# Two of the three column sums of each late pair move from Pool to the vector engine

## The chip, the cores and the metric

One core of a Trainium2 chip runs the whole program. The time is the device time of one execution in microseconds; the median of three runs is what is predicted. Names: TensorE (PE in the rows, PEld its weight loads), the vector engine (DVE), ScalarE (ACT), Pool (POOL), and SP, whose queue starts the DMAs.

## What is computed

A stack of four layers over 512 tokens of width 1024. The change lies in the last two layers, in the feed-forward block of each:

```python
h = rms_norm(x, norm_g[l, 2]) * (1.0 + sc2) + sh2
y = jnp.square(jax.nn.relu(h @ w_up[l])) @ w_down[l]      # w_up 1024x4096, w_down 4096x1024
x = x + gt2 * rms_norm(y, norm_g[l, 3])
```

Everything is float32, and the result must have float32's accuracy. The hidden size 4096 is the inner dimension of the product with `w_down`.

## The kernel before

Each float32 product is made of three reduced-precision ones: an operand is split into a high part (a rounded copy, made by ScalarE) and a low part (the operand less its high part, made by the vector engine), and TensorE adds high x high, low x high and high x low.

The feed-forward block of a layer runs in four chunks (`CHUNKS`, c = 0 to 3) of eight 128-wide tiles of the hidden size. In a chunk TensorE first makes the eight hidden tiles (L2551 to L2553), then the down projection of these 1024 rows of `w_down`. The down projection saves products: it is a two-by-two block product with seven multiplications in place of eight (the Winograd form), which needs sums and differences of blocks of the weights (column sums) and of the hidden activations (row sums). The seven multiplications are spread over eight steps w = 0 to 7 that the text calls pairs. Early pairs (0 to 3) and late pairs (4 to 7) have three products each, numbered i, in the order i = 2, 0, 1, each for two halves j = 0, 1, and a product is three matmuls of 128x512 (L3192 to L3194): 18 matmuls a pair. The seventh multiplication, 24 matmuls with the column differences of all late pairs (tile `col_diff`), closes the chunk.

For a late pair w the blocks of `w_down` lie in the tile `down_raw` (four blocks raw[:, 0] to raw[:, 3], one DMA of 1 MB from SP's queue, four buffers), and this is made of them:

- column difference t3 = raw3 - raw2, sum 1 = t3 + raw0, sum 2 = raw1 - sum 1: L1526, L1529 and L1532, all three on Pool, four pairs one after the other (`late_sums`). Sums 1 and 2 go to the tile `down_whole`, which shares its memory with `down_low`, so they wait for TensorE's products of pair w - 2.
- ScalarE (`late_high`, in this order): high part of raw3 (L1319), of t3 (L1321), and of both sums together, 128x1024 (L1323). It waits for the difference before the second and for sum 2 before the third.
- the vector engine: `late_block` (L2387), the low part of raw3, which product i = 2 needs; `late_low` (L2391), the low part of both sums, 128x1024, which products i = 0 and i = 1 need; and `diff_low` (L2394), the low part of t3, which only the seventh multiplication needs.

The prediction calls these three block-low, pair-low and difference-low.

The vector engine also adds finished products from PSUM to the sums in SBUF (L2400; in chunk 0 some are copies, L2402). These gathers free banks of PSUM: the two fifth sums (128x1024 each) must be done before pair 4's product i = 2, the two first sums (128x512 each; none in chunk 0, and in chunks 0 and 3 ScalarE also copies the bank, L1403) before pair 4's product i = 0; the two second sums come between pairs 6 and 7, the sixth after pair 7.

Nothing schedules this: every engine works through its own instructions in the order written, and semaphores hold it where an operand is missing. That order is the loop at the end of the vector engine's program, and the two `for` loops over w on ScalarE and Pool.

## Time and profile before

| | before |
|---|---|
| median of 3 runs | 1935.22 us (1934.49 to 1935.59) |
| profiled execution | 1937.91 us |
| its span, first to last instruction | 1936.1 us |
| TensorE matmul busy | 1843.9 us, 95% of the span |
| vector engine busy | 1439.1 us, 74% |
| ScalarE busy | 931.5 us, 48% |
| Pool busy | 277.0 us, 14% |
| granted TensorE clock, mean | 0.988 of full speed |

The first two rows are what was timed and the one execution that was profiled; 1.8 us of that execution lie outside its span. The busy rows are sums over the whole span and hide which stage waits for what; the rows shown further down come from the late pairs. In the chain of work that ended last, Pool has 5% of the span, on lines L1526, L1529 and L1532 above all; each of the eight chunks passes through them.

### The profile page before, as it was taken

How to read it: one execution, taken by the hardware profiler on the slowest of the kernel's cores; microseconds unless marked ns; L12 is line 12 of the kernel's file. 1: busy time of each engine (PE TensorE's matmuls, PEld its weight loads, DVE VectorE, ACT ScalarE, POOL GpSimd, SP SyncE). 2: the span in 40 equal slices, each digit the busy share in tenths (PEclk: the TensorE clock that was granted, in tenths of full speed). 3: DMA queues.
4: the chain of work that ended last, by engine and by line, in shares of the span. 5: the costliest groups of instructions: out<-in, count | busy, mean ns of one | idle time of the engine just before them, and what ended most of it. 6: DMA issues, size and time to landing. Idle time of an engine off the chain costs nothing.

```text
span 1936.1 us, 25511 instructions
## 1 busy us (share of the span) xinstructions
PE 1843.9 (95%) x9594; PEld 1438.4 (74%) x9594; DVE 1439.1 (74%) x2286; ACT 931.5 (48%) x1581; POOL 277.0 (14%) x194
## 2 busy tenths in 40 slices
PE   6999998999899999999999999999999999999997
PEld 3777566887566777777987777877777898778785
DVE  5797668886698897756876758684754687585878
ACT  4554544333323345466654544554455665445364
POOL 0002100000201111000013314340000003140514
PEclk9999999999999999999999999999999999999999
DMA  9466035886001452111232424232211213242432
GB/s 363 181 226 253 1 114 201 313 328 222 8 9 39 175 193 109 66 66 67 76 132 99 152 104 178 89 153 102 95 66 45 88 61 136 103 176 93 151 136 102
DMA packets 50016, 255.07 MB, mean 132 GB/s; under 512 B 5513, under 2 KB 7562, under 8 KB 31596
## 3 DMA queue, kind: packets, MB, share of 16 engines
q1 hardware_dynamic: 49900, 253.53, 35.4%
q8 instruction: 72, 1.18, 0.2%
q14 instruction: 44, 0.36, 0.1%
HBM read 251.28 MB, written 2.10 MB: 131 GB/s over the span
## 4 chain that ended last, share of the span: by engine, by line
PE 68%; DVE 16%; POOL 5%; ACT 5%; issue 4%; DMA 2%; POOLq 0%; SPq 0%; DVEq 0%; ACTq 0%
PE banks L2551 9%; PE banks L2552 9%; PE banks L2553 9%; PE banks L2921 3%; PE banks L2923 3%; PE banks L2922 3%; PE banks L2815 3%; PE banks L3192 3%; PE banks L3194 2%; PE banks L3193 2%; PE banks L2835 2%; POOL down_whole L1529 2%; POOL down_whole L1532 2%; PE banks L2736 2%; POOL col_diff L1526 2%
## 5 line engine op out<-in xcount | busy, mean ns | idle before, releaser
L2551 PE MATMUL banks<-h_high,w_high 128*128 128x512 f32 x888 | 349.7, 394 | 11.7 <-DVE w_low L1561 7.9
L2552 PE MATMUL banks<-h_low,w_high 128*128 128x512 f32 x888 | 346.6, 390 | 0.0
L2553 PE MATMUL banks<-h_high,w_low 128*128 128x512 f32 x888 | 346.5, 390 | 0.0
L2551 PEld LDWEIGHTS banks<-h_high,w_high 128*128 128x128 f32 x888 | 167.3, 188 | 53.8 <-DVE w_low L1561 12.5
L2553 PEld LDWEIGHTS banks<-h_high,w_low 128*128 128x128 f32 x888 | 167.2, 188 | 35.0
L2552 PEld LDWEIGHTS banks<-h_low,w_high 128*128 128x128 f32 x888 | 167.3, 188 | 35.0 <-issue 0.7
L1526 POOL TENSOR_TENSOR col_diff<-down_raw 128x512 f32<-128x512 f32 x32 | 53.7, 1677 | 674.8 <-DMA down_raw<-in_wd 674.8
L1576 DVE CUSTOM_DVE_ANT_0 mod_raw<-mod_raw,cond_row 128x1024 f32<-128x1024 f32 x112 | 131.5, 1219 | 2.5 <-DMA mod_raw<-in_wmod 2.4
L2921 PE MATMUL banks<-h_high,w_high 128*128 128x512 f32 x288 | 115.2, 400 | 2.5 <-DVE w_low L2025 1.7
L2923 PE MATMUL banks<-h_high,w_low 128*128 128x512 f32 x288 | 112.3, 390 | 0.0
L2922 PE MATMUL banks<-h_low,w_high 128*128 128x512 f32 x288 | 112.2, 390 | 0.0
L1561 DVE TENSOR_TENSOR w_low<-w_raw,w_high 128x1024 fp32r<-128x1024 f32 x66 | 80.6, 1221 | 41.2 <-ACT w_high L632 41.1
L3192 PE MATMUL banks<-down_high,row_sums_high 128*128 128x512 f32 x192 | 80.9, 422 | 19.7 <-DVE down_low L2391 8.6
L632 ACT ACTIVATE w_high<-w_raw 128x1024 fp32r<-128x1024 f32 x66 | 69.8, 1058 | 48.1 <-DMA w_raw<-in_wt 27.4
L2334 DVE TENSOR_TENSOR w_low<-w_raw,w_high 128x1024 fp32r<-128x1024 f32 x49 | 64.3, 1311 | 26.2 <-ACT w_high L1271 26.2
L2109 DVE TENSOR_REDUCE stats<-banks 128x2 f32<-128x1024 f32 (+3 forms) x32 | 25.6, 822 | 74.5 <-PE banks L2952 63.2
L1278 ACT ACTIVATE relu<-banks 128x512 f32<-128x512 f32 x52 | 30.9, 594 | 99.0 <-PE banks L2553 99.0
L1323 ACT ACTIVATE down_high<-down_whole 128x1024 fp32r<-128x1024 f32 x32 | 33.9, 1060 | 90.3 <-POOL down_whole L1532 90.0
L2025 DVE TENSOR_TENSOR w_low<-w_raw,w_high 128x1024 fp32r<-128x1024 f32 x38 | 47.5, 1251 | 39.9 <-ACT w_high L981 30.1
L1271 ACT ACTIVATE w_high<-w_raw 128x1024 fp32r<-128x1024 f32 x49 | 51.3, 1048 | 52.9 <-PE banks L3194 52.9
L3193 PE MATMUL banks<-down_low,row_sums_high 128*128 128x512 f32 x192 | 75.2, 391 | 0.0
L3194 PE MATMUL banks<-down_high,row_sums_low 128*128 128x512 f32 x192 | 75.1, 391 | 0.0
(590 smaller groups left out, 4617.4 us busy)
## 6 DMA issues: line engine op xcount, KB each, us to landing
w_raw<-in_wt SPq DMA_DIRECT2D x96, 1024.0 KB, 4.9
mod_raw<-in_wmod SPq DMA_DIRECT2D x128, 512.0 KB, 5.0
down_raw<-in_wd SPq DMA_DIRECT2D x32, 1024.0 KB, 7.2
down_raw<-in_wd SPq DMA_DIRECT2D x32, 768.0 KB, 4.2
mod_first<-in_wmod SPq DMA_DIRECT2D x8, 1024.0 KB, 10.6
cmp_w<-in_cmp_w SPq DMA_DIRECT2D x4, 1024.0 KB, 6.9
x<-in_xT SPq DMA_DIRECT2D x2, 1024.0 KB, 6.6
dft<-in_dft SPq DMA_DIRECT2D x2, 1024.0 KB, 7.5
```

Of the source, the lines that this page charges most:

```text
L1526: gp.tensor_tensor(t3[:, :], raw[:, 3, :], raw[:, 2, :], sub).then_inc(*did(f"mix_s.{c}.{w}.0"))
L1561: v.tensor_tensor(low[:, :, :].rearrange("p k c -> p (k c)"), RAW[b // 2][:, b % 2, :], high[:, :, :].rearrange("p k c -> p (k c)").bitcas ...
L1576: v.tensor_tensor_reduce(w, w, row[:, :], 1.0, 0.0, mul, add, sums[:, k:k + 1]).then_inc(mod_used, 1)
L2551: mm(out, high[:, k, :], H[:, k, :], start=k == order[0], stop=False)
L2552: mm(out, high[:, k, :], L[:, k, :], start=False, stop=False)
L2553: last = mm(out, low[:, k, :], H[:, k, :], start=False, stop=k == order[-1])
L2921: mm(out, WH[t % 2][:, k, :], Hh[:, k, :], start=k == 0, stop=False)
L2922: mm(out, WH[t % 2][:, k, :], Hl[:, k, :], start=False, stop=False)
L2923: last = mm(out, WL[t % 2][:, k, :], Hh[:, k, :], start=False, stop=k == KT - 1)
L3192: mm(out, rh, wh, start=start, stop=False)
L3193: mm(out, rh, wl, start=False, stop=False)
L3194: return mm(out, rl, wh, start=False, stop=stop)
```

## The change

Pool keeps the first of its three instructions for each late pair, the column difference (`late_diff`). The two sums are now issued by the vector engine, in a new function with the old name. In the vector engine's order they stand right behind `late_block` of the same pair, and `diff_low` is moved to stand behind them, ahead of `late_low`; it now waits for ScalarE's copy of the difference by a wait of its own. For pair 4 all this comes ahead of the fifth sums. The operands, the tiles and what is computed stay the same, and TensorE, ScalarE and SP issue what they did.

```diff
-            def late_sums(c, w):
-                raw, t3, out = BLOCKS[RAW_OF[w]], T3f[w % PK], OPf[w % 2]
+            def late_diff(c, w):
+                raw, t3 = BLOCKS[RAW_OF[w]], T3f[w % PK]
                 pool.wait_ge(*when(f"blocks{RAW_OF[w]}.{c}.{w}"))
...
                 gp.tensor_tensor(t3[:, :], raw[:, 3, :], raw[:, 2, :], sub).then_inc(*did(f"mix_s.{c}.{w}.0"))
-                pool.wait_ge(*when(f"mix_s.{c}.{w}.0"))
-                pool.wait_ge(*when(f"mix_p.{c}.{w - 2}.0.1"))
-                gp.tensor_tensor(out[:, 0, :], t3[:, :], raw[:, 0, :], add).then_inc(*did(f"mix_s.{c}.{w}.1"))
-                pool.wait_ge(*when(f"mix_s.{c}.{w}.1"))
-                pool.wait_ge(*when(f"mix_p.{c}.{w - 2}.1.1"))
-                gp.tensor_tensor(out[:, 1, :], raw[:, 1, :], out[:, 0, :], sub).then_inc(*did(f"mix_s.{c}.{w}.2"))
...
                 for w in range(PK, 8):
-                    late_sums(c, w)
+                    late_diff(c, w)
...
+            def late_sums(c, w):
+                raw, t3, out = BLOCKS[RAW_OF[w]], T3f[w % PK], OPf[w % 2]
+                dve.wait_ge(*when(f"mix_s.{c}.{w}.0"))
+                dve.wait_ge(*when(f"mix_p.{c}.{w - 2}.0.1"))
+                v.tensor_tensor(out[:, 0, :], t3[:, :], raw[:, 0, :], add).then_inc(*did(f"mix_s.{c}.{w}.1"))
+                dve.wait_ge(*when(f"mix_s.{c}.{w}.1"))
+                dve.wait_ge(*when(f"mix_p.{c}.{w - 2}.1.1"))
+                v.tensor_tensor(out[:, 1, :], raw[:, 1, :], out[:, 0, :], sub).then_inc(*did(f"mix_s.{c}.{w}.2"))
...
             def diff_low(c, w):
+                dve.wait_ge(*when(f"mix_h.{c}.{w}.1"))
...
                 late_block(c, 4)
+                late_sums(c, 4)
+                diff_low(c, 4)
                 for j in range(2):
                     fifth_sum(c, j)
                 late_low(c, 4)
                 for j in range(2):
                     first_sum(c, j)
-                diff_low(c, 4)
                 for w in range(5, 8):
                     late_block(c, w)
+                    late_sums(c, w)
+                    diff_low(c, w)
                     late_low(c, w)
-                    diff_low(c, w)
```

How the instructions stand on the vector engine in chunk 1, from block-low of pair 4 to pair-low of pair 5, before the change (`y_tokens` from banks are the fifth sums, `sq` from banks the first sums):

```order
L2387 TENSOR_TENSOR down_low_200<-down_raw_218,down_high_198 128x512 [waits mix_on_scalar]
L2400 TENSOR_TENSOR y_tokens_220<-y_tokens_220,banks 128x2x512 [waits y_on_vector,mix_on_tensor] x2
L2391 TENSOR_TENSOR down_low_200<-down_whole_202,down_high_198 128x1024 [waits mix_on_scalar]
L2400 TENSOR_TENSOR sq_118<-sq_118,banks 128x512 [waits y_on_scalar,mix_on_tensor]
L2400 TENSOR_TENSOR sq_119<-sq_119,banks 128x512 [waits y_on_scalar,mix_on_tensor]
L2394 TENSOR_TENSOR col_diff_low_208<-col_diff_212,col_diff_high_204 128x512
L2387 TENSOR_TENSOR down_low_201<-down_raw_217,down_high_199 128x512 [waits mix_on_scalar]
L2391 TENSOR_TENSOR down_low_201<-down_whole_203,down_high_199 128x1024 [waits mix_on_scalar]
```

and the same stretch after it, where the line numbers have shifted (block-low is L2390, the sums L2383 and L2386, difference-low L2398, pair-low L2394, the gathers L2404):

```order
L2390 TENSOR_TENSOR down_low_200<-down_raw_218,down_high_198 128x512 [waits mix_on_scalar]
L2383 TENSOR_TENSOR down_whole_202<-col_diff_212,down_raw_218 128x512 [waits mix_on_tensor,mix_on_gpsimd]
L2386 TENSOR_TENSOR down_whole_202<-down_raw_218,down_whole_202 128x512 [waits mix_on_tensor,mix_on_vector]
L2398 TENSOR_TENSOR col_diff_low_208<-col_diff_212,col_diff_high_204 128x512 [waits mix_on_scalar]
L2404 TENSOR_TENSOR y_tokens_220<-y_tokens_220,banks 128x2x512 [waits y_on_vector,mix_on_tensor] x2
L2394 TENSOR_TENSOR down_low_200<-down_whole_202,down_high_198 128x1024 [waits mix_on_scalar]
L2404 TENSOR_TENSOR sq_118<-sq_118,banks 128x512 [waits y_on_scalar,mix_on_tensor]
L2404 TENSOR_TENSOR sq_119<-sq_119,banks 128x512 [waits y_on_scalar,mix_on_tensor]
L2390 TENSOR_TENSOR down_low_201<-down_raw_217,down_high_199 128x512 [waits mix_on_scalar]
L2383 TENSOR_TENSOR down_whole_203<-col_diff_213,down_raw_217 128x512 [waits mix_on_tensor,mix_on_gpsimd]
L2386 TENSOR_TENSOR down_whole_203<-down_raw_217,down_whole_203 128x512 [waits mix_on_tensor,mix_on_vector]
L2398 TENSOR_TENSOR col_diff_low_209<-col_diff_213,col_diff_high_205 128x512 [waits mix_on_scalar]
```

Three instructions have come between block-low of pair 4 and the fifth sums, one of them with a wait for Pool.

On Pool, pairs 4 and 5 of the same chunk before the change:

```order
L1526 TENSOR_TENSOR col_diff_212<-down_raw_218 128x512 [waits mix_on_tensor,hid_on_vector,blocks2]
L1529 TENSOR_TENSOR down_whole_202<-col_diff_212,down_raw_218 128x512 [waits mix_on_tensor,mix_on_gpsimd]
L1532 TENSOR_TENSOR down_whole_202<-down_raw_218,down_whole_202 128x512 [waits mix_on_tensor,mix_on_gpsimd]
L1526 TENSOR_TENSOR col_diff_213<-down_raw_217 128x512 [waits mix_on_tensor,blocks1]
L1529 TENSOR_TENSOR down_whole_203<-col_diff_213,down_raw_217 128x512 [waits mix_on_tensor,mix_on_gpsimd]
```

and after it, pair 4 of chunk 1 to pair 4 of chunk 2:

```order
L1526 TENSOR_TENSOR col_diff_212<-down_raw_218 128x512 [waits mix_on_tensor,hid_on_vector,blocks2]
L1526 TENSOR_TENSOR col_diff_213<-down_raw_217 128x512 [waits mix_on_tensor,blocks1]
L1526 TENSOR_TENSOR col_diff_214<-down_raw_216 128x512 [waits mix_on_tensor,blocks0]
L1526 TENSOR_TENSOR col_diff_215<-down_raw_219 128x512 [waits mix_on_tensor,blocks3]
L1526 TENSOR_TENSOR col_diff_212<-down_raw_218 128x512 [waits mix_on_tensor,hid_on_vector,blocks2]
```

The four differences of a chunk now stand back to back, each held only by its block's DMA and, for pairs 6 and 7, by the first product of pair 3.

## Rows read from the trace of the kernel before

**Rows 1.** The waits between 1085 and 1125 us: waiting, awaited, total us, times, longest

```profile
ACT down_high L1323 <- POOL down_whole L1532: 12.2, 4, 3.3
```

**Rows 2.** The timeline of TensorE, chunk 1, pair 4 and pair 7: start us, us

```profile
1103.86 0.39 PE L3192 MATMUL banks<-down_high,row_sums_high 128*128 128x512 f32 x1
...
1104.99 0.39 PE L3194 MATMUL banks<-down_high,row_sums_low 128*128 128x512 f32 x1
1105.72 0.47 PE L3192 MATMUL banks<-down_high,row_sums_high 128*128 128x512 f32 x1 [0.35 <-DVE sq L2400]
...
1121.61 0.50 PE L3192 MATMUL banks<-down_high,row_sums_high 128*128 128x512 f32 x1
```

**Rows 3.** The timeline of Pool, chunk 1, pairs 4 to 7

```profile
1097.77 1.78 POOL L1526 TENSOR_TENSOR col_diff<-down_raw 128x512 f32<-128x512 f32 x1 [64.47 <-DMA down_raw<-in_wd]
...
1101.33 1.30 POOL L1532 TENSOR_TENSOR down_whole<-down_raw,down_whole 128x512 f32<-128x512 f32 x1
...
1107.89 1.75 POOL L1526 TENSOR_TENSOR col_diff<-down_raw 128x512 f32<-128x512 f32 x1
1109.72 2.15 POOL L1529 TENSOR_TENSOR down_whole<-col_diff,down_raw 128x512 f32<-128x512 f32 x1
1111.95 1.62 POOL L1532 TENSOR_TENSOR down_whole<-down_raw,down_whole 128x512 f32<-128x512 f32 x1
1113.53 1.74 POOL L1526 TENSOR_TENSOR col_diff<-down_raw 128x512 f32<-128x512 f32 x1
```

**Rows 4.** The timeline of the vector engine, chunk 1, pairs 4 and 5

```profile
1098.39 1.71 DVE L2387 TENSOR_TENSOR down_low<-down_raw,down_high 128x512 fp32r<-128x512 f32 x1
1100.66 2.35 DVE L2400 TENSOR_TENSOR y_tokens<-y_tokens,banks 128x1024 f32<-128x1024 f32 x2 [0.56 <-PE banks L3194]
1103.76 1.23 DVE L2391 TENSOR_TENSOR down_low<-down_whole,down_high 128x1024 fp32r<-128x1024 f32 x1 [0.74 <-ACT down_high L1323]
1104.90 1.28 DVE L2400 TENSOR_TENSOR sq<-sq,banks 128x512 f32<-128x512 f32 x2
...
1109.05 1.66 DVE L2391 TENSOR_TENSOR down_low<-down_whole,down_high 128x1024 fp32r<-128x1024 f32 x1 [0.58 <-ACT down_high L1323]
1110.64 1.78 DVE L2394 TENSOR_TENSOR col_diff_low<-col_diff,col_diff_high 128x512 fp32r<-128x512 f32 x1
```

**Rows 5.** The timeline of ScalarE, chunk 1, pair 5

```profile
1107.96 1.06 ACT L1323 ACTIVATE down_high<-down_whole 128x1024 fp32r<-128x1024 f32 x1 [3.20 <-POOL down_whole L1532]
```

**Rows 6.** DMA issues, 1098 to 1099 us (pair 7's block): KB, us to landing

```profile
down_raw<-in_wd SPq DMA_DIRECT2D x1, 1024.0 KB, 6.6
```

**Rows 7.** Chunks 2 and 3: SP's request, its landing, and the timeline of TensorE

```profile
1185.42 0.33 SPq L614 DMA_DIRECT2D down_raw<-in_wd  x1
...
down_raw<-in_wd SPq DMA_DIRECT2D x1, 1024.0 KB, 6.9
...
1190.89 0.39 PE L3194 MATMUL banks<-down_high,row_sums_low 128*128 128x512 f32 x1
1191.35 0.47 PE L3192 MATMUL banks<-down_high,row_sums_high 128*128 128x512 f32 x1
...
1207.23 0.50 PE L3192 MATMUL banks<-down_high,row_sums_high 128*128 128x512 f32 x1
...
1278.23 0.47 PE L3192 MATMUL banks<-down_high,row_sums_high 128*128 128x512 f32 x1 [0.70 <-ACT sq L1403]
...
1293.48 0.50 PE L3192 MATMUL banks<-down_high,row_sums_high 128*128 128x512 f32 x1
```

**Rows 8.** Chunk 0: the timeline of Pool, the vector engine and TensorE

```profile
1011.22 2.86 POOL L1526 TENSOR_TENSOR col_diff<-down_raw 128x512 f32<-128x512 f32 x1 [167.77 <-DMA down_raw<-in_wd]
...
1012.24 0.69 DVE L2387 TENSOR_TENSOR down_low<-down_raw,down_high 128x512 fp32r<-128x512 f32 x1
...
1019.23 0.50 PE L3192 MATMUL banks<-down_high,row_sums_high 128*128 128x512 f32 x1 [0.24 <-DVE down_low L2391]
...
1035.70 0.50 PE L3192 MATMUL banks<-down_high,row_sums_high 128*128 128x512 f32 x1
```

## The prediction

> **What bounds the kernel now.** I read the table of busy shares first: TensorE is busy 95% of the span, so a change elsewhere gains only where TensorE stands still. Then the list of waits over the down projection of the first layer's chunk 1 [rows 1]: ScalarE waits 12.2 us for Pool's third column sum, more than anything waits for anything else inside the late pairs. That chain (Pool's three sums, ScalarE's high parts, the vector engine's low parts, TensorE) paces the late pairs 4 to 7. TensorE's own rows give the size [rows 2]. Undisturbed, matmuls start (1104.99 - 1103.86) / 5 = 0.226 us apart. From the first matmul of pair 4 to the product of pair 7 that uses its column sums there are 60 matmuls, 13.6 us of work, and they take 1121.61 - 1103.86 = 17.75 us. So 4.1 us are lost in this chunk, and some 33 us in eight chunks (two layers of four): that is the ceiling of a gain.
>
> **Why a pair takes 5.6 us.** Pool starts one pair's first difference at 1107.89 and the next one's at 1113.53: a period of 5.64 us [rows 3]. TensorE needs 18 x 0.226 = 4.08 us for a pair. Pool's rows alternate with the vector engine's. L2391 alone takes 1.23 us [rows 4] and a 128x512 one such as L2387 0.69 [rows 8]; beside Pool L2391 takes 1.66 and L2394 1.78 [rows 4]. The ends show the pattern: L2391 ends at 1110.71, Pool's L1529, issued at 1109.72, ends 1.16 later at 1111.87, L2394, issued at 1110.64, ends 0.55 later at 1112.42, Pool's L1532 another 1.15 later. Only one of the two engines runs such an instruction at a time. One pair holds this turn for 3 x 1.15 + 2 x 0.55 + 1.08 = 5.63 us, which is the period. The gathers from PSUM are free of it: two of 128x1024 take 2.35 us at 1100.66 while Pool works [rows 3, 4].
>
> **Part 1, pairs 5 to 7: a gain.** The vector engine now runs per pair: block-low (L2387 of before), sum 1, sum 2, difference-low, pair-low. Of independent ones the next starts 0.08 before the last ends: the two at 1104.90 take 0.68 each and 1.28 together [rows 4], so those of 0.68 us start 0.60 apart. Sum 2 needs sum 1's result: 0.68 + 0.04 = 0.72. After sum 2 ScalarE makes the high part in 1.06 [rows 5], with 0.03 and 0.04 of handing over, while difference-low runs. Pair-low (1.23) then occupies 1.14 until the next start (1103.76 to 1104.90, rows 4). The period is 0.60 + 0.72 + 0.68 + 0.03 + 1.06 + 0.04 + 1.14 = 4.27 us, if Pool's differences are out of the way. The pair-low of a pair ends 4.36 after its block-low starts. The two second-sum gathers between pairs 6 and 7 add 1.20. So the product with pair 7's sums starts 2 x 4.27 + 1.20 + 4.36 + 0.05 = 14.15 us after pair 5's block-low starts. Three saved periods are worth 3 x 1.36 = 4.1 us; but the gathers, which Pool's pace hid before, now count.
>
> **Part 2, pair 4: a loss.** Here two sums and a wait for Pool are put ahead of the gathers, and TensorE needs the gathers' bank for its very first product of pair 4. Chunk 1, on the clock of before: Pool's first difference ends at 1099.55 (1097.77 + 1.78) and block-low at 1100.10 (1098.39 + 1.71) [rows 3, 4]. Sum 1 follows to 1100.70. Pool, rid of its sums, goes straight to pair 5's difference, whose block I take as landed; it has its turn 1100.70 to 1101.85, so sum 2 ends at 1102.40. Difference-low ends at 1103.00, the two fifth sums run 1102.92 to 1105.27. TensorE wanted pair 4 at 1103.86; it starts its first product at 1104.15, its second at 1105.3 and is done with both at 1106.1. Meanwhile pair 7's block lands: it is requested as pair 4's block-low begins (1098.4) and takes 6.6 us [rows 6], so Pool's last difference asks at 1105.05, just ahead of pair-low at 1105.19. Pool goes first, to 1106.35, and pair-low ends at 1107.43. The first of the two first sums frees the next bank at 1108.03, and TensorE goes on at 1108.08, where before it did at 1105.72 [rows 2]: 2.36 us later.
>
> **Sum per chunk.** Chunk 1: pair 5's block-low starts at 1107.35 + 1.20 = 1108.55; plus 14.15 gives 1122.70 against 1121.61 [rows 2]: +1.1 us. After that product nothing in the chunk differs, since the sixth sums and the products of the column differences wait for it in both, so this is the chunk's whole change. Chunk 2: the last block is requested at 1185.42 and takes 6.9 [rows 7], to 1192.3, after pair-low has begun (about 1191.1); one turn fewer, which is 1.03 us (1106.35 less the 1105.32 at which pair-low would have had the turn). The delay at pair 4 is 2.36 - 1.03 + 0.27 (before stood less there: 1190.89 to 1191.35 against 1104.99 to 1105.72, rows 2 and 7) = 1.6; from there 14.7 instead of 1207.23 - 1191.35 = 15.88 [rows 7]: +0.4. Chunk 3: ScalarE copies bank A twice behind the first sums, in both kernels, so the delay at pair 4 is that of chunk 2, 1.6; but the copies (0.6 each) also stand ahead of pair 5's high part, and from pair 4's product on it is 14.15 + 0.47 + 0.65 = 15.3 against 1293.48 - 1278.23 = 15.25 [rows 7]: +1.7. Chunk 0: Pool's first difference took 2.86 and ended at 1014.08 [rows 8]. Sum 1 waits for it, then the same row of events, with two of Pool's differences in between and the fifth sums last at 1020.6, puts TensorE at 1021.77 against 1019.23: +2.5. There are no first sums in this chunk, so 14.05 follow against 1035.70 - 1019.23 = 16.47: +0.1. One layer: 0.1 + 1.1 + 0.4 + 1.7 = 3.3; I take the second as the first: 6.6 us. SP's queue is not in it: its block loads for pairs 5 to 7 wait for early pairs, the next weights for difference-low of pair 6, which comes earlier. The added wait for ScalarE before difference-low costs nothing: that copy is done two instructions before.
>
> The profiled execution was 1937.91 (span 1936.1), the median of the runs 1935.22; the sum goes on both: 1944.5 profiled, **1941.8** for the median.
>
> **Against two rules of the Trainium skill.** Pool's difference in chunk 0 was issued at 1011.22, while a 128x512 vector instruction that began at 1012.24 still went ahead of it [rows 8]. "SBUF — State Buffer", section "Who interferes with whom", says that whoever starts first gets the shared port pair for the whole instruction. The rows of chunk 1 agree with it; this one doesn't. By that rule the difference would here end 1.2 us sooner, the sums of chunk 0 with it, and the total would be 6.6 - 2 x 1.2 = 4.2: 1939.4. "Perfetto Trace Analysis", section "Optimizing Scalar/DVE Operations", says that moving work between the two engines might not help, as they share a read port. In this kernel the turn per pair falls from 5.63 to 1.15 + 4 x 0.55 + 1.08 = 4.43 us, so it helps in the steady pairs; that the total doesn't gain comes from the order at pair 4.
>
> **Rivals.**
> - *Gain wins (faster).* The cost at pair 4 hangs on Pool's differences getting turns between the vector engine's instructions. If the blocks land so that all of them fall under gathers from PSUM or waits, chunk 1 and chunk 0 lose two turns of 1.03 each, chunks 2 and 3 one: six a layer, twelve in all, -12.4. 6.6 - 12.4 = -5.8: 1929.4. It decides from about seven turns saved. For it: gathers and Pool do run side by side [rows 3, 4]. Against: the vector engine has no gap between 1098.4 and 1105.
> - *Draw.* Four or five of the twelve turns go that way, above all the near tie of 0.14 us at 1105.05 to 1105.19: 6.6 - 5 = +1.6, 1936.8.
> - *One more turn a chunk (slower still).* A difference blocked at pair 4 comes again before block-low of pair 5: +8 x 1.03, 1950.
> - *First come, first served in chunk 0 too:* 1939.4, as above.
>
> **How the numbers follow.** Forecast 0.53; draw 0.23; gain wins 0.12; first come 0.05; one more turn 0.07. This kernel's measurement tells about 0.2% (3.9 us) from no change, so same is 1931.4 to 1939.1. The forecast case itself reaches from 1938 to 1946; 0.02 of it falls in same. Faster 0.12, same 0.25, slower 0.63. The range leaves out the two outer cases (0.19): 1933 to 1946.5.
>
> **What would show it.** Right: Pool's rows at L1526 only, some of them above 1.3 us; pairs 5 to 7 at a period near 4.3 us; TensorE at pair 4 waiting for fifth sums and then about 2 us for pair-low; the chunk's product with pair 7's sums about 1 us later than before. Wrong: pair-low of pair 4 ending within 1 us of its old place (then the gain wins), or a period of the steady pairs above 4.6 us (then it is slower than 1945). It also fails if the chunk's loss is taken up later, by a wait of TensorE in the next chunk that shrinks; I see none there.

## The result: 6.7 us slower, and the profile after

| | before | after |
|---|---|---|
| median of 7 runs each | 1935.62 us | 1942.36 us |
| lowest to highest | 1934.49 to 1938.26 | 1939.93 to 1943.77 |
| profiled execution, its span | 1937.91, 1936.1 us | 1943.77, 1941.9 us |
| TensorE's time lost in the late pairs, eight chunks | 34.1 us | 41.0 us |
| granted TensorE clock, mean | 0.988 | 0.984 |

The ratio is 1.0030, with a 95% interval from 1.0021 to 1.0039. The "time lost" is the measure of the rest of this document: from TensorE's timeline, every distance between two starts of matmuls that is over 0.25 us, less the undisturbed 0.227 us, summed over the 30.5 us ahead of each chunk's first product with the column differences.

From the page of the kernel after (busy times, then the shares of the chain that ended last, then two groups of instructions with busy us, mean ns, and idle time before them with what ended it):

```profile
PE 1844.7 (95%) x9594; PEld 1446.0 (74%) x9594; DVE 1442.4 (74%) x2350; ACT 929.3 (48%) x1581; POOL 160.4 (8%) x130
...
PE 70%; DVE 19%; ACT 5%; issue 4%; DMA 1%; POOL 0%; SPq 0%; DVEq 0%; ACTq 0%; POOLq 0%
...
L1526 POOL TENSOR_TENSOR col_diff<-down_raw 128x512 f32<-128x512 f32 x32 | 51.5, 1611 | 751.2 <-DMA down_raw<-in_wd 708.4
...
L1323 ACT ACTIVATE down_high<-down_whole 128x1024 fp32r<-128x1024 f32 x32 | 34.0, 1061 | 93.8 <-DVE down_whole L2386 93.8
```

Pool's busy time fell by 117 us and it left the chain (5% to 0%), but the vector engine, with 64 more instructions, has only 3 us more busy time: its new instructions took the place of stretching by Pool: the median block-low went from 1.77 to 0.68 us, and the median difference-low too. What ScalarE waits for changed its name, not its size: the third sum, now the vector engine's L2386, where it was Pool's with 12.2 us in [rows 1]. The same view for the late pairs of that chunk, 1100 to 1125 us (waiting, awaited, total us, times, longest):

```profile
ACT down_high L1323 <- DVE down_whole L2386: 12.9, 4, 5.0
```

The vector engine in chunk 1, pairs 4 to 7, where [rows 4] stood (start us, us):

```profile
1097.97 1.72 DVE L2390 TENSOR_TENSOR down_low<-down_raw,down_high 128x512 fp32r<-128x512 f32 x1
1099.61 0.68 DVE L2383 TENSOR_TENSOR down_whole<-col_diff,down_raw 128x512 f32<-128x512 f32 x1
1100.33 1.76 DVE L2386 TENSOR_TENSOR down_whole<-down_raw,down_whole 128x512 f32<-128x512 f32 x1
1102.01 0.68 DVE L2398 TENSOR_TENSOR col_diff_low<-col_diff,col_diff_high 128x512 fp32r<-128x512 f32 x1
1102.61 2.34 DVE L2404 TENSOR_TENSOR y_tokens<-y_tokens,banks 128x1024 f32<-128x1024 f32 x2
1104.88 1.21 DVE L2394 TENSOR_TENSOR down_low<-down_whole,down_high 128x1024 fp32r<-128x1024 f32 x1
1106.01 1.27 DVE L2404 TENSOR_TENSOR sq<-sq,banks 128x512 f32<-128x512 f32 x2
1107.21 0.68 DVE L2390 TENSOR_TENSOR down_low<-down_raw,down_high 128x512 fp32r<-128x512 f32 x1
...
1110.34 1.23 DVE L2394 TENSOR_TENSOR down_low<-down_whole,down_high 128x1024 fp32r<-128x1024 f32 x1 [0.52 <-ACT down_high L1323]
...
1114.63 1.23 DVE L2394 TENSOR_TENSOR down_low<-down_whole,down_high 128x1024 fp32r<-128x1024 f32 x1 [0.53 <-ACT down_high L1323]
```

Pool in the same stretch, where [rows 3] stood:

```profile
1100.26 1.29 POOL L1526 TENSOR_TENSOR col_diff<-down_raw 128x512 f32<-128x512 f32 x1 [1.11 <-DMA down_raw<-in_wd]
...
1105.18 2.04 POOL L1526 TENSOR_TENSOR col_diff<-down_raw 128x512 f32<-128x512 f32 x1 [1.17 <-DMA down_raw<-in_wd]
```

And TensorE, where [rows 2] stood:

```profile
1103.97 0.47 PE L3198 MATMUL banks<-down_high,row_sums_high 128*128 128x512 f32 x1 [0.36 <-DVE y_tokens L2404]
...
1106.83 0.47 PE L3198 MATMUL banks<-down_high,row_sums_high 128*128 128x512 f32 x1 [0.86 <-DVE sq L2404]
...
1121.39 0.50 PE L3198 MATMUL banks<-down_high,row_sums_high 128*128 128x512 f32 x1 [1.11 <-DVE down_low L2394]
```

The pair-lows of pairs 5 and 6 start 4.29 us apart instead of 5.64. The entry is what got longer: TensorE waits for the fifth sums at 1103.97, for the first sums at 1106.83, and again ahead of 1121.39.

By chunk, TensorE's time lost:

| us | layer 1: chunk 0 | 1 | 2 | 3 | layer 2: chunk 0 | 1 | 2 | 3 | sum |
|---|---|---|---|---|---|---|---|---|---|
| before | 5.22 | 4.08 | 3.86 | 3.88 | 5.25 | 3.90 | 4.10 | 3.84 | 34.1 |
| after | 5.46 | 4.37 | 4.56 | 5.50 | 5.51 | 5.70 | 4.39 | 5.56 | 41.0 |
| change | +0.2 | +0.3 | +0.7 | +1.6 | +0.3 | +1.8 | +0.3 | +1.7 | +6.9 |
| forecast | +0.1 | +1.1 | +0.4 | +1.7 | +0.1 | +1.1 | +0.4 | +1.7 | +6.6 |

### The profile page after: what moved, and what is told of

Its sections match the earlier page's. It is cut to its first block, busy times and chain, and to the rows that moved or that the text cites. A ratio compares the mean times of both kernels' runs of the same rounds, so it can differ in the third digit from the quotient of the medians.

```text
span 1941.9 us, 25511 instructions
## 1 busy us (share of the span) xinstructions
PE 1844.7 (95%) x9594; PEld 1446.0 (74%) x9594; DVE 1442.4 (74%) x2350; ACT 929.3 (48%) x1581; POOL 160.4 (8%) x130
## 4 chain that ended last, share of the span: by engine, by line
PE 70%; DVE 19%; ACT 5%; issue 4%; DMA 1%; POOL 0%; SPq 0%; DVEq 0%; ACTq 0%; POOLq 0%
PE banks L2557 9%; PE banks L2559 9%; PE banks L2558 9%; PE banks L3198 3%; PE banks L2927 3%; PE banks L3200 3%; PE banks L3199 3%; PE banks L2929 3%; PE banks L2928 3%; PE banks L2821 3%; PE banks L2841 2%; PE banks L2742 2%; DVE mod_raw L1570 1%; PE banks L2956 1%; DVE down_low L2394 1%
## 5 line engine op out<-in xcount | busy, mean ns | idle before, releaser
L1526 POOL TENSOR_TENSOR col_diff<-down_raw 128x512 f32<-128x512 f32 x32 | 51.5, 1611 | 751.2 <-DMA down_raw<-in_wd 708.4
```

## Experiments

The theory: Pool's turns pace pairs 5 to 7 and their removal gains there, but at pair 4 the sums on the vector engine come into the one path that TensorE waits for. The rival theories are with each experiment. The lost time is split where pair 4's first product with its column sums starts: "to pair 4" is what lies ahead of that, "behind" what follows. Each time is compared with runs of the kernel before on the same chip (medians 1937.36, 1936.35, 1937.03 and 1937.17 us).

| kernel | median us | against before | ratio, 95% interval | lost to pair 4 | lost behind | both | between chunks |
|---|---|---|---|---|---|---|---|
| before | | | | 5.3 | 28.8 | 34.1 | 1.2 |
| after | 1942.36 | +6.7 | 1.0030 [1.0021, 1.0039] | 21.2 | 19.8 | 41.0 | 1.2 |
| pair 4 back on Pool | 1940.31 | +3.0 | 1.0017 [1.0008, 1.0026] | 5.7 | 32.3 | 38.0 | 1.2 |
| Pool without its reads | 1923.56 | -13.8 | 0.9930 [0.9917, 0.9943] | 5.4 | 18.0 | 23.4 | 1.2 |
| pair 4 alone on the vector engine | 1934.73 | -2.6 | 0.9988 [0.9980, 0.9997] | 19.6 | 10.7 | 30.3 | 1.2 |
| difference on the vector engine too | 1949.58 | +12.2 | 1.0066 [1.0053, 1.0079] | 9.0 | 39.5 | 48.5 | 1.1 |
| after, difference-lows late | 1928.73 | -7.6 | 0.9962 [0.9948, 0.9975] | 13.7 | 12.4 | 26.1 | 2.2 |
| pair 4 on Pool, difference-lows late | 1928.83 | -7.5 | 0.9964 [0.9952, 0.9976] | 6.7 | 20.1 | 26.8 | 2.2 |
| pairs 4 and 7 on the vector engine | 1927.71 | -8.6 | 0.9961 [0.9947, 0.9974] | 16.8 | 7.6 | 24.4 | 3.8 |
| filler matmuls | 1942.62 | +6.3 | 1.0031 [1.0020, 1.0042] | 16.4 | 11.8 | 28.2 | 1.2 |
| before, difference-lows late | 1935.48 | -1.6 | 0.9993 [0.9984, 1.0002] | 6.6 | 22.9 | 29.5 | 4.7 |
| fifth sums first | 1949.87 | +12.8 | 1.0067 [1.0055, 1.0079] | 30.0 | 19.0 | 49.0 | 1.2 |
| before, weights asked for earlier | 1934.45 | -2.7 | 0.9982 [0.9972, 0.9992] | 7.5 | 22.9 | 30.4 | 2.3 |
| split, difference-lows in the wait | 1931.30 | -5.9 | 0.9970 [0.9959, 0.9980] | 16.9 | 13.2 | 30.1 | 1.1 |

The change of the two right columns together gives that of the median within about 2 us in all rows but two. With the fillers it leaves out the fillers' own time, 48 x 0.227 = 10.9 us. Pool without its reads gained 3 us more than it shows, and the cause of that stays open.

### 1. Pair 4 back on Pool

Pool makes all three sums of pair 4, the vector engine has its old order there; pairs 5 to 7 as in the kernel after.

```diff
-                late_sums(c, 4)
-                diff_low(c, 4)
                 for j in range(2):
                     fifth_sum(c, j)
                 late_low(c, 4)
                 for j in range(2):
                     first_sum(c, j)
+                diff_low(c, 4)
```

> The changed kernel with pair 4 undone: pair 4's two sums are back on Pool and the vector engine has the old order there; pairs 5 to 7 stay as changed. My theory (the loss is made at pair 4, where two sums, a wait for Pool and Pool's turns at the vector engine come ahead of the gathers; pairs 5 to 7 gain): TensorE reaches pair 4's first sums product about where the kernel before did, one turn later at most (+1.1 us); from there 15.2 us follow in place of 15.9, so about +0.4 us a chunk, +3.5 us against before, 3 us less than the changed kernel. Rival (every sum on the vector engine costs the same wherever it stands): six of eight sums are still there, +5.0 us.

Measured: +3.0 us in the medians, +3.3 by the ratio; my number, though the interval (+1.5 to +5.0) just takes in the rival's +5.0. The loss didn't go, it moved by one pair. TensorE at pair 5 of chunk 1, and the vector engine ahead of it:

```profile
1103.29 0.69 DVE L2409 TENSOR_TENSOR col_diff_low<-col_diff,col_diff_high 128x512 fp32r<-128x512 f32 x1
1103.89 0.69 DVE L2401 TENSOR_TENSOR down_low<-down_raw,down_high 128x512 fp32r<-128x512 f32 x1
1104.49 1.79 DVE L2394 TENSOR_TENSOR down_whole<-col_diff,down_raw 128x512 f32<-128x512 f32 x1
...
1108.13 1.23 DVE L2405 TENSOR_TENSOR down_low<-down_whole,down_high 128x1024 fp32r<-128x1024 f32 x1 [0.52 <-ACT down_high L1323]
```

```profile
1106.90 0.39 PE L3216 MATMUL banks<-down_high,row_sums_low 128*128 128x512 f32 x1
1109.41 0.80 PE L3214 MATMUL banks<-down_high,row_sums_high 128*128 128x512 f32 x1 [2.13 <-DVE down_low L2405]
```

TensorE stood 2.51 us between these two starts, where it stood 0.99 in the kernel before. Pool, working ahead of the vector engine, had the sums of the next pair ready; the vector engine begins them only when it has finished the pair ahead. So the first pair whose sums are on the vector engine pays an entry, be it pair 4 or pair 5: the time lost up to pair 4's sums falls to 5.7 us, near the 5.3 of before, and that behind it rises from 19.8 to 32.3.

### 2. Pool without its reads

Pool's difference is a fill with zeros: same wait, same write, no operand is read. The column difference is left out of the computation here.

```diff
-                gp.tensor_tensor(t3[:, :], raw[:, 3, :], raw[:, 2, :], sub).then_inc(*did(f"mix_s.{c}.{w}.0"))
+                gp.memset(t3[:, :], 0.0).then_inc(*did(f"mix_s.{c}.{w}.0"))
```

> The changed kernel, but Pool fills the column difference with zeros in place of subtracting two blocks: the difference is left out of the computation, every wait and every other instruction stays. Pool then writes and reads nothing. My theory (turns between the two engines, taken by Pool's reading instructions, make a good part of the loss): no vector instruction is stretched beside Pool any more; 1 to 3 us less a chunk than the changed kernel, -9 us against before. The Trainium skill (SBUF: State Buffer, section Who interferes with whom) says that a vector instruction with two SBUF inputs contends only with a Pool instruction that reads SBUF; by it the rows of 0.68 us stay at 0.68. Rival (the vector engine's load alone): as the changed kernel, +6.7 us.

Measured: -13.8 us against before (I had -9), so 20 less than the kernel after. The vector engine at pair 4 of chunk 1, and one of Pool's fills under it:

```profile
1094.70 0.69 DVE L2383 TENSOR_TENSOR down_whole<-col_diff,down_raw 128x512 f32<-128x512 f32 x1
1095.43 0.69 DVE L2386 TENSOR_TENSOR down_whole<-down_raw,down_whole 128x512 f32<-128x512 f32 x1
1096.04 0.68 DVE L2398 TENSOR_TENSOR col_diff_low<-col_diff,col_diff_high 128x512 fp32r<-128x512 f32 x1
```

```profile
1095.93 0.53 POOL L1526 MEMSET col_diff<- 128x512 f32 x1 [1.95 <-DMA down_raw<-in_wd]
```

The fill ran from 1095.93 to 1096.46 beside two instructions that kept their 0.69 and 0.68; in the kernel after the row at this place took 1.76. So the entry's cost is the turns that Pool's differences take, together with the time of the differences themselves (1.79 against 0.53). All of the entry goes with them: the time lost up to pair 4's sums is 5.4 us, against 21.2 in the kernel after and 5.3 before. The Trainium skill, "SBUF — State Buffer", section "Who interferes with whom", says that a vector instruction with two operands in SBUF contends with a Pool instruction that reads SBUF, and not with one that only writes it; the trace agrees.

### 3. Pair 4 alone on the vector engine

On Pool, and on the vector engine (in its loop over pairs 5 to 7 the sums are gone):

```diff
                     late_diff(c, w)
+                    if w in (5, 6, 7):
+                        late_sums(c, w)
...
                 for w in range(5, 8):
                     late_block(c, w)
-                    late_sums(c, w)
-                    diff_low(c, w)
                     late_low(c, w)
+                    diff_low(c, w)
```

> The other part alone: pair 4's sums on the vector engine in the new order, pairs 5 to 7 with all three instructions on Pool in the old one. My theory: pair 4 is late by some 2 us as in the changed kernel, but Pool, rid of pair 4's sums, starts pair 5 so much earlier that the old pace of 5.64 us ends near the old place: -1.4 us against before (-4 to +3). Rival (every sum on the vector engine costs the same): two of eight, +1.7 us.

Measured: -2.6 us (-2.3 by the ratio); the sign and, within the interval, the size of the theory. The rival, that every sum on the vector engine costs the same (+1.7), falls. Pool goes ahead with pair 5 while the vector engine does pair 4, and pair 5's pair-low follows pair 4's by 3.15 us (1103.14 to 1106.29) where it took 5.29 before. Up to pair 4's sums this kernel loses nearly what the kernel after does (19.6 against 21.2 us), so the prediction's "part 2, a loss" stands; but behind them it loses 10.7 against 19.8. In the order that the change chose, pair 4 on the vector engine is a loss on the whole where pair 5 must follow on the same engine, and not where it doesn't.

```profile
1103.14 1.43 DVE L2405 TENSOR_TENSOR down_low<-down_whole,down_high 128x1024 fp32r<-128x1024 f32 x1
...
1106.29 1.21 DVE L2405 TENSOR_TENSOR down_low<-down_whole,down_high 128x1024 fp32r<-128x1024 f32 x1
```

### 4. The difference on the vector engine too

```diff
                 late_block(c, 4)
+                late_diff(c, 4)
                 late_sums(c, 4)
```

and the same for pairs 5 to 7; Pool does nothing in the late pairs.

> One step further: the column difference too goes to the vector engine, right behind block-low; Pool has nothing in the late pairs. My theory (the vector engine's own work ahead of the gathers counts; the turns are only part): its period is 0.6 longer, 4.9 us, so 2 us more in pairs 5 to 7, less what the turns cost at pair 4: +9.6 us against before. Rival (turns alone are the loss): without Pool there are none and the kernel is faster than before, some -5 us.

Measured: +12.2 us, 2.6 more than I had. No row is stretched any more, but the chain of one pair has a fifth instruction in it: the pair-lows of pairs 5 and 6 start 5.01 us apart. An instruction of 0.69, whose result the next one needs, makes every pair 0.72 us longer; on Pool the four differences took turns around pair 4 alone. There this kernel loses only 9.0 us, 12 less than the kernel after, so most of the entry of 16 us was turns; behind it it loses 20 more.

```profile
1109.51 1.23 DVE L2403 TENSOR_TENSOR down_low<-down_whole,down_high 128x1024 fp32r<-128x1024 f32 x1 [0.53 <-ACT down_high L1323]
...
1114.52 1.23 DVE L2403 TENSOR_TENSOR down_low<-down_whole,down_high 128x1024 fp32r<-128x1024 f32 x1 [0.53 <-ACT down_high L1323]
```

### 5. After, with the difference-lows late

The sums stay where the change put them. Difference-low of pair 4 goes into the wait for ScalarE at pair 5, the second sums into the one at pair 6, difference-low of pair 5 into that of pair 7, the last two behind everything.

```diff
-                diff_low(c, 4)
...
+                late_block(c, 5)
+                late_sums(c, 5)
+                diff_low(c, 4)
+                late_low(c, 5)
+                late_block(c, 6)
+                late_sums(c, 6)
+                for j in range(2):
+                    second_sum(c, j)
+                late_low(c, 6)
+                late_block(c, 7)
+                late_sums(c, 7)
+                diff_low(c, 5)
+                late_low(c, 7)
+                diff_low(c, 6)
+                diff_low(c, 7)
```

> The changed kernel with only the vector engine's order altered: difference-low of pair 4 goes from ahead of the fifth sums into pair 5's wait for ScalarE, difference-low of 5 into pair 7's, those of 6 and 7 to the end, and the second sums into pair 6's wait. Pool and the split of the work stay as changed. My theory (the changed kernel loses by what stands ahead of the gathers and of pair-low, not by who adds): pair-low of pair 4 ends 0.6 us sooner, the second sums cost nothing: 1 to 2 us less a chunk than the changed kernel, -7 us against before. Rival (the load counts, wherever it stands): as the changed kernel, +6.7 us.

Measured: -7.6 us, my number, 14 less than the kernel after, with the same instructions on the same engines. Half of the gain lies up to pair 4's sums (13.7 us lost instead of 21.2), where difference-low no longer stands ahead of the fifth sums, and half behind them (12.4 instead of 19.8). The second sums now lie under ScalarE's high part:

```profile
1110.60 0.69 DVE L2386 TENSOR_TENSOR down_whole<-down_raw,down_whole 128x512 f32<-128x512 f32 x1
1111.21 1.28 DVE L2404 TENSOR_TENSOR y_tokens<-y_tokens,banks 128x512 f32<-128x512 f32 x2
1112.42 1.22 DVE L2394 TENSOR_TENSOR down_low<-down_whole,down_high 128x1024 fp32r<-128x1024 f32 x1
```

The pair-lows of pairs 6 and 7 start 4.28 apart (1112.42 to 1116.70), where the kernel after has 5.48 (1114.63 to 1120.11).

### 6. Pair 4 on Pool, difference-lows late

Experiments 1 and 5 together: the difference-lows and second sums as in experiment 5, and at pair 4

```diff
-                late_sums(c, 4)
                 for j in range(2):
                     fifth_sum(c, j)
                 late_low(c, 4)
```

> The same order, and pair 4's two sums back on Pool. My theory: -10 us against before, 3 us less than the one with pair 4 on the vector engine. Rival (load): +5 us.

Measured: -7.5 us, 2.5 short, and no better than experiment 5. The two gains don't add: TensorE still waits 2 us or so at pair 5 (1107.60 to 1109.53 in chunk 1), the entry of experiment 1.

### 7. Pairs 4 and 7 on the vector engine, 5 and 6 on Pool

On Pool, and the vector engine's order (the first line taken out stood ahead of the fifth sums, the rest stands behind the first sums):

```diff
                     late_diff(c, w)
+                    if w in (5, 6):
+                        late_sums(c, w)
...
-                diff_low(c, 4)
...
-                for w in range(5, 8):
...
+                late_block(c, 5)
+                late_low(c, 5)
+                late_block(c, 6)
+                late_low(c, 6)
+                late_block(c, 7)
+                late_sums(c, 7)
+                diff_low(c, 4)
+                for j in range(2):
+                    second_sum(c, j)
+                late_low(c, 7)
+                diff_low(c, 5)
+                diff_low(c, 6)
+                diff_low(c, 7)
```

> The sums divided: pairs 4 and 7 on the vector engine, 5 and 6 on Pool, with three of the differences' low parts at the end of the late pairs. Pool, free of pair 4, is early with pair 5's sums, so both engines bring pairs in turn. My theory: 1.2 to 2 us less a chunk than before, -14 us. Rival (load): four of eight sums, +3.3 us.

Measured: -8.6 us (-7.6 by the ratio), the fastest median of all kernels that compute the whole result, though its interval overlaps those of experiments 5 and 6, and 5 to 6 short of my number. The late pairs gave 9.7 us; 2.6 were lost again between the chunks, and in three chunks a stretch at TensorE's lower clock came behind a wait of 2 us (below).

### 8. Filler matmuls

After the change TensorE's matmuls start 0.427 us apart for about 4 us behind its longest waits. Six matmuls without use are put into the wait at pair 4, and the wait that guards their bank goes ahead of them.

```diff
-                        if i == 1 and w == PK:
+                        if i == 0 and w == PK:
                             pe.wait_ge(taken, U + PER_CHUNK * c + 8 + PRIME)
+                            for _ in range(6):
+                                mm(bank(BANK_F), A2h[:, 1, 0, 0:P], A2h[:, 1, 0:2, :].rearrange("p n c -> p (n c)"), start=True, stop=True)
```

> The changed kernel with six matmuls of 128x512 (1.4 us, into a bank that is free there) put into TensorE's wait between pair 4's first products and its sums' products. In the changed kernel's trace some chunks show matmuls 0.427 us apart in place of 0.227 for some 4 us behind a wait of 2 us or more. My theory: in these chunks TensorE waits for pair 5's pair-low anyway, so the slower stretch costs nearly nothing; with the filler the 0.427 go away in the chunks whose wait lies there, and the time stays within 2 us of the changed kernel (+5 to +9 against before). Rival (the slower stretch adds 0.2 us a matmul to the chunk, about 2 us in each of five chunks): up to 10 us less than the changed kernel, -3 against before.

Measured: +6.3 us, the time of the kernel after, as the theory said; the rival (-3) falls. The wide spacing was gone in chunks 1 to 3 of both layers and the time didn't move. In two of them where the spacing had been wide, and where one turn fell at pair 4 with the fillers as without (chunk 2, and chunk 3 of the second layer), the lost time with the fillers' own 1.36 us is 4.3 and 5.5 us, against 4.6 and 5.5 in the kernel after. So there the slow stretch costs next to nothing: TensorE would wait for pair 5's pair-low anyway.

### 9. Before, with the difference-lows late

All sums on Pool, and only the vector engine's order changed (against the kernel before).

```diff
-                diff_low(c, 4)
-                for w in range(5, 8):
...
+                late_block(c, 5)
+                late_low(c, 5)
+                late_block(c, 6)
+                late_low(c, 6)
+                for j in range(2):
+                    second_sum(c, j)
+                late_block(c, 7)
+                diff_low(c, 4)
+                late_low(c, 7)
+                diff_low(c, 5)
+                diff_low(c, 6)
+                diff_low(c, 7)
```

> All three sums of every late pair stay on Pool, as in the kernel before; the only change is in the vector engine's order: each pair's difference-low runs later, where the vector engine would otherwise stand waiting for ScalarE (the last three of them behind pair 7's pair-low), and the second sums likewise. My theory: where difference-low stands is a lever of its own, because it then takes no turn from Pool's sums while TensorE waits for them; my schedule gives -6 us against before (about 1930). Rival: the gain of the version with this order and the sums on the vector engine came from the move of the sums alone; then this is 0 +- 2 against before, since Pool's three turns a pair still pace pairs 5 to 7 (period near 5.6 less 0.5 at most).

Measured: -1.6 us, 0.9993 [0.9984, 1.0002]: no difference that can be told. That is the rival's number, and the period is the rival's too (5.6 less 0.5 at most): it fell from 5.64 to 5.20. What neither had is that this was a gain, given back elsewhere:

```profile
1106.49 1.29 POOL L1526 TENSOR_TENSOR col_diff<-down_raw 128x512 f32<-128x512 f32 x1
1107.86 2.17 POOL L1532 TENSOR_TENSOR down_whole<-col_diff,down_raw 128x512 f32<-128x512 f32 x1
1110.11 1.62 POOL L1535 TENSOR_TENSOR down_whole<-down_raw,down_whole 128x512 f32<-128x512 f32 x1
1111.69 1.29 POOL L1526 TENSOR_TENSOR col_diff<-down_raw 128x512 f32<-128x512 f32 x1
```

The late pairs lost 4.6 us less. 3.5 of them were given back between the chunks, in the hidden tiles of the next one:

```profile
1224.25 0.39 PE L2572 MATMUL banks<-h_high,w_low 128*128 128x512 f32 x1
1225.93 0.47 PE L2570 MATMUL banks<-h_high,w_high 128*128 128x512 f32 x1 [1.29 <-issue]
```

SP asks for the next chunk's weights after pair 6's difference-low. That request came 1.68 us ahead of the chunk's first product with the column differences, where the kernel before has 6.41.

### 10. Before, with the weights asked for earlier

Experiment 9 with pair 6's difference-low in the place of pair 4's.

```diff
                 late_block(c, 7)
-                diff_low(c, 4)
+                diff_low(c, 6)
                 late_low(c, 7)
+                diff_low(c, 4)
                 diff_low(c, 5)
-                diff_low(c, 6)
                 diff_low(c, 7)
```

> The version with all sums on Pool and late difference-lows, with one more swap: pair 6's difference-low takes the place of pair 4's (ahead of pair 7's pair-low, no longer behind it). SP requests the next chunk's first weights only after pair 6's difference-low. Theory: late difference-lows shortened the late pairs by 4.6 us in eight chunks (TensorE's lost time 34.1 to 29.5) and gave 3.5 back, since the request came at 1120.62 in chunk 1 instead of 1118.07 and TensorE then waited in the next hidden tiles (4.7 us between the chunks instead of 1.2). With the request back near 1118 the 3.5 are kept: 1935.5 - 3.5 = 1932. Rival: the time between the chunks has nothing to do with the request (code or another block): 1935.5 +- 1.5 as before the swap.

Measured: -2.7 us (-3.5 by the ratio). The request came 4.70 us ahead, and the time between the chunks fell from 4.7 to 2.3 us: the cause is the request, and two thirds of what I expected came back. One chunk lost a turn instead, so the total moved by 1 to 2 us, which the two intervals don't tell apart.

### 11. The fifth sums first

```diff
                 late_block(c, 4)
+                for j in range(2):
+                    fifth_sum(c, j)
                 late_sums(c, 4)
                 diff_low(c, 4)
-                for j in range(2):
-                    fifth_sum(c, j)
```

> The changed kernel with one change: at pair 4 the two fifth sums come ahead of the two column sums and of difference-low (block-low, fifth sums, sum 1, sum 2, difference-low, pair-low). My theory: the column sums then end later and ScalarE's high part with them, which nothing covers any more, so pair-low of pair 4 comes about 1.3 us later than in the changed kernel in every chunk while TensorE's first product of pair 4 is no longer late; +1.0 to +1.3 a chunk, +8 to +10 us over the changed kernel (about 1951). Rival: the fault of the change is that it put three instructions ahead of the gathers; putting the gathers back in front then gives back what pair 4 lost, -4 to -7 us against the changed kernel (1935 to 1938, no slower than before).

Measured: +12.8 us, 6 more than the kernel after; the theory said 8 to 10, the rival a gain. TensorE has its bank at once, runs on, and then stands 4.02 us:

```profile
1102.44 0.39 PE L3200 MATMUL banks<-down_high,row_sums_low 128*128 128x512 f32 x1
1106.46 0.76 PE L3198 MATMUL banks<-down_high,row_sums_high 128*128 128x512 f32 x1 [3.63 <-DVE sq L2404]
```

From Pool's first difference to this product it is 10.51 us (1095.95 to 1106.46), in the kernel after 9.48 (1097.35 to 1106.83). So the order at pair 4 that the change chose is the better of the two, and the loss doesn't come from the fifth sums standing behind the column sums. With the fifth sums first, the column sums end later, and pair-low waits 0.52 us for ScalarE's high part, which the fifth sums covered in the kernel after.

### 12. The split, with difference-lows in the wait

In experiment 7 the vector engine stands idle for 4.37 us ahead of pair 6's pair-low.

```diff
                 late_block(c, 6)
+                diff_low(c, 4)
+                diff_low(c, 5)
                 late_low(c, 6)
                 late_block(c, 7)
                 late_sums(c, 7)
-                diff_low(c, 4)
+                diff_low(c, 6)
                 for j in range(2):
                     second_sum(c, j)
                 late_low(c, 7)
-                diff_low(c, 5)
-                diff_low(c, 6)
                 diff_low(c, 7)
```

> The fastest version so far (sums of pairs 4 and 7 on the vector engine, of 5 and 6 on Pool), with the difference-lows of pairs 4 and 5 put into the vector engine's 4.4 us wait ahead of pair 6's pair-low, and pair 6's ahead of pair 7's pair-low, so that SP's request for the next weights comes about 3.5 us earlier. Theory: the 3.8 us between the chunks go back to 1.2 and the late pairs stay at 24.4: 1927.7 - 2.6 = 1925, low enough to beat every version. Rival: the two instructions put into the wait take turns from Pool's second sum of pair 6, which ScalarE and pair-low wait for: +1.08 in each chunk, +8.6 less 2.6, so 1933 to 1934.

Measured: -5.9 us, nearer to the rival and 2 to 3 worse than experiment 7. The two intervals overlap, but the time lost in the late pairs went from 24.4 to 30.1 us. The idle time was Pool's turn. The vector engine and Pool at pair 6 of chunk 1:

```profile
1108.25 3.48 DVE L2409 TENSOR_TENSOR col_diff_low<-col_diff,col_diff_high 128x512 fp32r<-128x512 f32 x2
1111.65 1.21 DVE L2405 TENSOR_TENSOR down_low<-down_whole,down_high 128x1024 fp32r<-128x1024 f32 x1
```

```profile
1107.86 1.62 POOL L1535 TENSOR_TENSOR down_whole<-down_raw,down_whole 128x512 f32<-128x512 f32 x1
1109.44 1.75 POOL L1526 TENSOR_TENSOR col_diff<-down_raw 128x512 f32<-128x512 f32 x1
```

Two instructions of 0.68 took 3.48 us and stretched Pool's two from 1.30 to 1.62 and 1.75. The time between the chunks did go back, from 3.8 to 1.1.

## Why the prediction was right, step by step

The mechanism held, in both of its parts. Up to pair 4's first product with its sums the prediction's terms give 2 x (2.5 + 2.4 + 1.6 + 1.6), about +16 us, and behind it about -9.5; measured +15.9 and -9.0. That the single chunks add up so well is in part luck, as the steps show.

- **What bounds it.** The 4.1 us lost in chunk 1 and the chain behind them hold: in the table the time follows TensorE's lost time in the late pairs in every kernel.
- **Part 1, the steady pairs.** Forecast a period of 4.27 us, measured 4.29; from pair 5's block-low to the product with pair 7's sums forecast 14.15, measured 14.18 (1107.21 to 1121.39). The turn explains both directions: experiment 2 (no turn, no stretching) and experiment 12 (two more turns).
- **Part 2, pair 4.** Forecast that TensorE goes on with the sums' product 2.36 us later in chunk 1; measured by the time lost up to there, 1.5 in the first layer (2.00 against 0.50) and 3.1 in the second (3.30 against 0.22). This is the term that was off. In the first layer the cause is one step: "pair 7's block ... takes 6.6 us, so Pool's last difference asks at 1105.05, just ahead of pair-low at 1105.19". In the kernel after the block took 7.1:

```profile
down_raw<-in_wd SPq DMA_DIRECT2D x1, 1024.0 KB, 7.1
```

  Pool asked at 1105.18, pair-low had begun at 1104.88, and it was Pool that waited (2.04 instead of 1.29). In the second layer the tie fell as the prediction had it: Pool asked first, at 1726.23, and pair-low took 2.08.

```profile
1726.51 2.08 DVE L2394 TENSOR_TENSOR down_low<-down_whole,down_high 128x1024 fp32r<-128x1024 f32 x1
```

  The 0.7 us too little there have another cause. Pool's first difference, issued at 1718.65, let two instructions of the vector engine pass, as in chunk 0, so sum 1 waited for it and TensorE lost 0.95 us at the fifth sums in place of 0.52; and the kernel before had stood 0.3 us less at this place than in the first layer.

```profile
1721.20 1.80 DVE L2383 TENSOR_TENSOR down_whole<-col_diff,down_raw 128x512 f32<-128x512 f32 x1 [1.18 <-POOL col_diff L1526]
```

  The prediction had the near tie among its rivals ("draw") but in the sum it gave both layers the same outcome. The errors, -0.8 and +0.7, come from two different places, and that they cancelled is luck.
- **Chunk 3** (+1.7; measured +1.6 and +1.7) and **chunk 0** (+0.1; +0.2 and +0.3) came as worked out, chunk 0 with Pool's first difference losing its turn again (2.9 and 2.8 us later at pair 4 where 2.5 were forecast, and 13.7 instead of 14.05 us from there). So the first-come rival is out: Pool's difference, issued at 1010.57, let the vector engine's next two instructions go ahead, and sum 1 began only at 1013.62:

```profile
1011.76 0.68 DVE L2390 TENSOR_TENSOR down_low<-down_raw,down_high 128x512 fp32r<-128x512 f32 x1
1013.62 1.76 DVE L2383 TENSOR_TENSOR down_whole<-col_diff,down_raw 128x512 f32<-128x512 f32 x1 [1.18 <-POOL col_diff L1526]
```

  **Chunk 2** was forecast +0.4 and measured +0.7 and +0.3, but not with the turns of the forecast. In the first layer sum 2 lost no turn (0.69), and pair-low lost one (2.32) to Pool's third difference, issued 0.04 us ahead of it. In the second layer neither lost one; sum 1 of pair 5 did (1.78).
- **The two rules of the Trainium skill.** That whoever starts first gets the port pair ("SBUF — State Buffer", "Who interferes with whom") doesn't fit Pool's first row of chunk 0 after the change either, nor that of chunk 1 in the second layer, and fits the tie of pair 4 in both layers. That moving work between these two engines might not help ("Perfetto Trace Analysis", "Optimizing Scalar/DVE Operations"): it lost 6.7 us in one order and gained 7.6 in another.
- **What the profile was to show.** Pool's rows at L1526 only, several above 1.3 us (mean 1.61): yes. Waits for the fifth sums, then for pair-low: yes, save that chunk 2 has none for the fifth sums, and the second one 0.9 to 2.1 us where about 2 were named. The wrong signs, pair-low of pair 4 within 1 us of its old place or a period above 4.6, didn't show, save in chunk 2 of layer 2, where the sums' product came only 0.45 us later than before. No chunk's loss was taken up later.
- **The rivals.** "Gain wins" needed seven turns saved; against the forecast one was saved in chunk 1 of the first layer, and one in chunk 2 of the second, where it came back at pair 5. "One more turn a chunk" showed in that chunk alone. The sum of +6.6 stands against +6.9 in the lost time, +5.8 in the spans and +6.7 in the medians.
- **What was too coarse.** The prediction ascribed the loss to three instructions ahead of the fifth sums. It isn't their place there: putting the fifth sums first loses more (experiment 11, 30.0 us up to pair 4's sums in place of 21.2). The loss there is mostly turns: 5.4 us with Pool's reads gone (experiment 2), 9.0 with the difference on the vector engine (experiment 4). And whether a loss at pair 4 is paid back is decided behind it. Experiments 3 and 7 lose 19.6 and 16.8 us there and are faster than before all the same, since Pool makes pair 5's sums meanwhile; with pair 4 back on Pool (experiment 1) the loss moves to pair 5. What costs, in the order that the change chose, is the first pair that has both its own sums and its successor's on the vector engine. The order of the rest counts as much: with the difference-lows and the second sums put off, the same move of sums gains 7.6 us (experiment 5). Neither does it alone: the move alone is +6.7, the late difference-lows alone -1.6. What the second sums give by themselves no run shows; experiment 9 left them between pairs 6 and 7.

## What to carry to other kernels

When two engines take turns, as the vector engine and Pool do here, count a move in turns as well as in busy time, and then ask what the slower engine did ahead of need: work moved from an engine that ran ahead to one that works pair by pair comes onto the path once per entry into the stage. Fill the waits of the engine that got the work with whatever nobody is waiting for, but look first whether that idle time is the other engine's turn, and which later DMA request hangs on the instruction that is put off. A near tie of 0.1 us between two engines should enter a sum as half of each outcome.

## What the runs showed of the hardware that I had not expected

**TensorE's clock behind a wait.** In chunk 2 of the kernel after TensorE stood from 1190.66 to 1192.94, and from the fourth matmul behind it they started 0.43 us apart:

```profile
1193.48 0.57 PE L3200 MATMUL banks<-down_high,row_sums_low 128*128 128x512 f32 x1
1193.85 0.63 PE L3198 MATMUL banks<-down_high,row_sums_high 128*128 128x512 f32 x1
1194.28 0.63 PE L3199 MATMUL banks<-down_low,row_sums_high 128*128 128x512 f32 x1
```

The granted clock from 1189 to 1191 us and behind that wait. Each row has the stretch and its length, the busy us and instructions of PE, PEld, DVE, ACT and POOL, the granted clock (1.00, then 0.58), the DMA share and GB/s:

```profile
1189.00:1191.00 2.00, 2.00 (x10) 1.35 (x8) 2.00 (x2) 0.51 (x1) 1.18 (x1) 1.00 0.31 131
1192.90:1196.90 4.00, 3.96 (x11) 3.13 (x12) 3.44 (x6) 1.45 (x2) 0.65 (x1) 0.58 0.00 0
```

That is the lower of its two levels, 1.2 GHz, for most of the stretch, and full speed again from 1197. Five of the eight chunks of the kernel after show it. It isn't decided by the length of the wait alone: in experiment 7 a wait of 2.01 us in chunk 1 was followed by it, and in experiment 12 one of 2.00 at the same place was not, nor was one of 3.18 in chunk 0 of experiment 11. Where nothing waits behind it, it costs: in experiment 7 the chunks with it lost 3.7, 3.7 and 4.4 us, those without 2.2 to 2.8. What decides it stays open.

**Who gets the turn.** Between the two engines the one that asked first went first in the other rows shown. Pool's first difference after a long idle time is an exception in chunk 0: it let later vector instructions pass before the change [rows 8] and after it. In the second layer's chunk 1 it did so too, in six of the kernels (2.5 to 3.2 us for the one row), the kernel after among them.
